# A transformer layer pair and a hybrid layer on one core: VectorE makes all low parts of the first block, a one-operation mask, and a new order of calls

## The chip, the cores and the metric

The kernel runs on one core of a Trainium2 chip. The metric is the device time of one execution in microseconds (us). Its engines are TensorE (PE, matmuls and transposes into eight PSUM banks), VectorE (DVE), ScalarE (ACT), GpSimd (POOL) and SyncE (SP, which here issues the loads). Each runs its own instruction list strictly in order, and they wait for each other through semaphores. DVE and ACT read PSUM; POOL doesn't.

## The reference

Two blocks in a row on 256 positions of 1024 columns, all in float32. The first block is two transformer layers:

```python
h = rms_norm(x, attn_norm_g[l]);  proj = h @ w_in[l]          # 1024 x 3656
# rotary q/k with a norm per head, then three mixers of 4 heads each:
moba = softmax(causal(q k)) v                                  # one block of 256: plain causal
diff = rms_norm((softmax(q1 k1) - lam * softmax(q2 k2)) v)     # differential
# dsa: per query the top 64 causal keys by an indexer of 8 heads, softmax over those
score = sum_h iw[h] * relu(iq[h] ik);  _, sel = top_k(causal(score), 64)
x = x + concat(moba, diff, dsa) @ w_out[l]
x = x + (silu(h2 @ w_gate[l]) * (h2 @ w_up[l])) @ w_down[l]    # 2816 wide, h2 = rms_norm(x)
```

The second block is one hybrid layer: `z = h @ w_in_2`, a gated MLP over positions (`y_a`, with a layer norm), 16 heads of compressed, selected and window attention (`y_b`), a convolution and linear recurrence (`y_c`), then

```python
merged = sum_i sigmoid(mg_i) * (y_i @ w_br_i)
x = x + rms_norm_2(merged @ w_o, g_post_mix)
x = x + rms_norm_2((silu(f_gate) * f_up) @ w_ffn_out, g_post_ffn)   # f from rms_norm_2(x)
```

## The kernel before

**Three products for one.** A weight chunk of 128 x 2048 floats (4 k-tiles of 512 columns, 1 MB) is loaded by SP into `raw`. ACT rounds it to `whi` (`split_hi`, called `hi` in the first block and `hi2` in the second), and DVE subtracts to get the rest, `wlo` (`split_lo`, called `lo` and `lo2`). The activations, transposed by TensorE, are split alike into `_hi` (ACT, `turned_hi_copy`) and `_lo` (DVE, `turned_lo_copy`) of `hT`, `mixT` and `ffT`. `three` then issues hi x hi, hi x lo and lo x hi (lines 587, 588, 589). `raw`, `whi` and `wlo` are rings of three slots: chunk i is loaded when the low part of chunk i-3 is done, and rounded when TensorE has used chunk i-3. `lo_ready` counts low parts, `used` counts chunks used up.

**First block.** Each engine's list for a layer is written out by hand as a row of calls, and their order is the schedule. On TensorE `row_product(p, j, r)` is a quarter of projection p (k-half j, rows r of 128; 12 matmuls), `turn_heads(s, b)` transposes heads, `index_scores` makes the indexer's scores, `group_scores`, `group_turn` and `group_values` are attention group g = 0 to 3 (scores, transposed probabilities, values; 1 and 2 differential, 3 the one with the top 64 keys), `mix_turn(h, r)` transposes the mixers' outputs and `out_product(n, j, r)` multiplies them by `w_out`, from chunks 17 to 20. ACT copies (`copy_z`, `heads_copy`), exponentiates (`attend_exp`) and normalises (`square_heads`, `scale_heads`). POOL rotates (`rotate`). DVE masks (`attend_mask`, three tiles), picks the top keys (`topk_rounds(a, b)` in 8 rounds, `topk_mask`), and blends (`blend`, `diff_norm`). Of the low parts, POOL makes those of chunks 18 and 20 (line 548, `pool_lo`), and DVE passes their completion on with `lo_from_pool`. `topk_mask` is two operations:

```python
dve(eng.tensor_scalar(chosen[:, :], index[:, :], TAKEN / 2, NEG, ALU.is_gt, ALU.mult))   # line 1804
dve(eng.tensor_tensor(chosen[:, :], chosen[:, :], causal[:, :], ALU.add))                # line 1806
```

**Second block.** Product b has chunks (b, 0) and (b, 1), which TensorE consumes with `product_chunk(b, j)`, each for rows 0 and then rows 1 (24 matmuls). Products 13 to 19 alternate with attention groups i (`attend_turn` transposes their probabilities; DVE's `attend_copy` moves a third of these to SBUF); `mix_positions(r)` is the MLP over positions and waits for the layer norm that DVE finishes at line 2341. Product 13 reads `mixT` (half 0 of its k-tiles in (13, 0), half 1 in (13, 1)) and waits for all four low parts of it (`turned_lo` 32). Around products 23 to 25 DVE does the recurrence (lines 2404 to 2421), which ends in `yc_lo`, the low part of `y_c`. Product 29 is the second half of `w_o`: its banks are freed by DVE's `gained(n, r, ...)` (line 1703), which needs `both_gain`, the product of two gain rows, and `x` times a gain. POOL makes these (lines 576 and 578) once the gain row is loaded (`ffn_gain`, SP line 454, behind all loads of products up to 29) and `yc_lo` has come. Then `post_square` (ACT), `new_rows` (DVE, line 2450) and `turn_row_part` (TensorE, line 631) give the rows of the last feed-forward part, `ffn`. Its result leaves through `gain` products (line 1950), `post_add` (line 1903) and four stores.

## Time and profile before

| | |
|---|---|
| median of 3 runs | 1286.12 us (1285.91 to 1287.7) |
| profiled execution, its own time | 1285.88 us |
| its span, first to last instruction | 1283.9 us |
| outside the span | 1.98 us |
| mean granted TensorE clock | 0.993 of full speed |
| HBM read | 211.28 MB, 165 GB/s over the span |
| chain that ended last | PE 86%, DVE 5%, issue 4%, ACT 2%, DMA 1%, POOL 1% |

Times in the profile count from the span's start. TensorE's busy time is modelled: matmuls overlap, so a row's duration is longer than the distance from one matmul's start to the next, and what is lost shows as idle time in square brackets ahead of an instruction, with what ended it behind the arrow. The chain is followed back from the last instruction, at each step to what released it.

### The profile page before, as it was taken

To read this page: it belongs to the slowest core of one execution; us is meant where nothing else is said; L and a number is where in the kernel's file an instruction comes from. 1 tells how busy PE (TensorE), PEld (TensorE's weight loads), DVE (VectorE), ACT (ScalarE), POOL (GpSimd) and SP (SyncE) were. 2 spreads that over 40 slices of the span, in tenths; PEclk is the share of its full clock that TensorE was granted. 3 is DMA by queue.
4 is the path that set the end of the run, shared out by engine and by line. 5 is a ranking of instruction groups with operands and counts; after the bars stand their busy time and mean duration, and the time that the engine had idled before them with its cause. 6 is when DMAs were issued, how large, how long until landed. Compare 5 with 4: busy or idle time off the path is not lost.

```text
span 1283.9 us, 16912 instructions
## 1 busy us (share of the span) xinstructions
PE 1254.1 (98%) x6430; PEld 1057.1 (82%) x6430; DVE 820.9 (64%) x983; ACT 663.4 (52%) x981; POOL 194.3 (15%) x162
## 2 busy tenths in 40 slices
PE   8999999999999999999999999999999999999998
PEld 6788888888887878888888899788997777888886
DVE  5898655545669866455457655866695677655444
ACT  5667463444466755434445644644547655634443
POOL 4884100001188620000000000000000003000000
PEclk9999999999999999999999998999999999999999
DMA  7533355556353344555564562343334455455551
GB/s 262 185 100 120 131 210 187 192 194 208 132 197 103 125 151 163 213 178 193 193 211 155 215 211 109 122 144 103 121 112 167 152 188 214 169 178 192 196 200 45
DMA packets 34219, 213.12 MB, mean 166 GB/s; under 512 B 4305, under 2 KB 5585, under 8 KB 11506
## 3 DMA queue, kind: packets, MB, share of 16 engines
q1 hardware_dynamic: 34098, 212.21, 46.9%
q8 instruction: 38, 0.62, 0.2%
q14 instruction: 19, 0.16, 0.0%
q0 software_dynamic: 64, 0.13, 0.0%
HBM read 211.28 MB, written 1.05 MB: 165 GB/s over the span
## 4 chain that ended last, share of the span: by engine, by line
PE 86%; DVE 5%; issue 4%; ACT 2%; DMA 1%; POOL 1%; POOLq 0%; DVEq 0%; ACTq 0%
PE bank L587 24%; PE bank L589 24%; PE bank L588 23%; PE bank L1002 3%; PE bank L694 2%; PE bank L753 2%; DVE wlo L1686 2%; PE bank L841 1%; PE bank L713 1%; ACT whi L1228 1%; DMA raw<-in_w_values 1%; DVE z L2166 1%; PE bank L615 1%; PE bank L678 1%; PE bank L1112 1%
## 5 line engine op out<-in xcount | busy, mean ns | idle before, releaser
L1686 DVE TENSOR_TENSOR wlo<-raw,whi 128x2048 fp32r<-128x2048 f32 (+4 forms) x197 | 442.4, 2250 | 246.8 <-ACT whi L1228 245.7
L1228 ACT ACTIVATE whi<-raw 128x2048 fp32r<-128x2048 f32 (+5 forms) x201 | 369.1, 1842 | 131.7 <-PE bank L589 124.0
L587 PE MATMUL bank<-whi,hT_hi 128*128 128x512 f32 (+4 forms) x1040 | 407.3, 392 | 6.2 <-DVE wlo L1686 3.0
L589 PE MATMUL bank<-whi,hT_lo 128*128 128x512 f32 (+4 forms) x1040 | 398.2, 383 | 0.0
L588 PE MATMUL bank<-wlo,hT_hi 128*128 128x512 f32 (+4 forms) x1040 | 397.8, 382 | 0.0
L587 PEld LDWEIGHTS bank<-whi,hT_hi 128*128 128x128 f32 x1040 | 196.6, 189 | 45.7 <-issue 6.8
L589 PEld LDWEIGHTS bank<-whi,hT_lo 128*128 128x128 f32 x1040 | 196.4, 189 | 36.3
L588 PEld LDWEIGHTS bank<-wlo,hT_hi 128*128 128x128 f32 x1040 | 196.9, 189 | 32.9
L587 PE MATMUL bank<-whi,mixT_hi 128*128 128x512 f32 (+1 forms) x248 | 96.5, 389 | 7.6 <-issue 3.9
L589 PE MATMUL bank<-whi,mixT_lo 128*128 128x512 f32 (+1 forms) x248 | 94.6, 381 | 0.0
L588 PE MATMUL bank<-wlo,mixT_hi 128*128 128x512 f32 (+1 forms) x248 | 94.5, 381 | 0.0
L587 PE MATMUL bank<-whi,ffT_hi 128*128 128x512 f32 x240 | 93.7, 390 | 0.0
L589 PE MATMUL bank<-whi,ffT_lo 128*128 128x512 f32 x240 | 93.5, 390 | 0.0
L588 PE MATMUL bank<-wlo,ffT_hi 128*128 128x512 f32 x240 | 93.4, 389 | 0.0
L1351 ACT ACTIVATE sqr<-bank,ssq 128x256 f32<-128x256 f32 x66 | 31.1, 473 | 88.0 <-PE bank L589 88.0
L1360 ACT ACTIVATE ffT_hi<-bank 128x256 fp32r<-128x256 f32 x60 | 19.8, 382 | 101.0 <-PE bank L841 101.0
L587 PEld LDWEIGHTS bank<-whi,mixT_hi 128*128 128x128 f32 (+1 forms) x248 | 47.1, 190 | 18.0 <-issue 6.2
L1917 DVE SCALAR_TENSOR_TENSOR probs<-bank,ssq,sqr 128x256 f32<-128x256 f32 x66 | 31.4, 480 | 44.6 <-ACT sqr L1351 44.6
L589 PEld LDWEIGHTS bank<-whi,mixT_lo 128*128 128x128 f32 (+1 forms) x248 | 47.1, 190 | 9.0
L588 PEld LDWEIGHTS bank<-wlo,mixT_hi 128*128 128x128 f32 (+1 forms) x248 | 47.1, 190 | 8.0
L576 POOL TENSOR_TENSOR z<-x,headsT 128x1024 f32<-128x1024 f32 x2 | 6.9, 3462 | 309.0 <-DMA headsT<-in_rows 309.0
L589 PEld LDWEIGHTS bank<-whi,ffT_lo 128*128 128x128 f32 x240 | 45.1, 188 | 9.4
(284 smaller groups left out, 1509.4 us busy)
## 6 DMA issues: line engine op xcount, KB each, us to landing
raw<-in_ff_loop SPq DMA_DIRECT2D x90, 1024.0 KB, 4.8
raw<-in_w_groups SPq DMA_DIRECT2D x64, 1024.0 KB, 4.8
raw<-in_w_out SPq DMA_DIRECT2D x8, 1024.0 KB, 5.6
raw<-in_ff_first SPq DMA_DIRECT2D x6, 1024.0 KB, 4.8
raw<-in_w_values SPq DMA_DIRECT2D x8, 728.0 KB, 4.2
raw<-in_w_comp SPq DMA_DIRECT2D x4, 1024.0 KB, 6.9
raw<-in_ff_last SPq DMA_DIRECT2D x3, 1024.0 KB, 6.8
raw<-in_w_values SPq DMA_DIRECT2D x4, 736.0 KB, 7.4
```

The source lines that it names most:

```text
L587: eng.matmul(out, lhsT=hi, rhs=wh, start=start, stop=False)
L588: eng.matmul(out, lhsT=hi, rhs=wl, start=False, stop=False)
L589: return eng.matmul(out, lhsT=lo, rhs=wh, start=False, stop=stop)
L615: mm = eng.transpose(bank[6 + r][:, k * P:(k + 1) * P], src[:, r, c:c + P], ident[:, :])
L694: mm = eng.matmul(bank[2 + u][:, c:c + keys], lhsT=headsT[half, q(h), rows], rhs=headsT[half, k(h), 0:keys], start=True, stop=True)
L753: mm = eng.matmul(out, lhsT=probsT[:, r + kt, h * P:(h + 1) * P], rhs=v(kt, h), start=(kt == 0), stop=(kt == r))
L1002: mm = eng.matmul(out, lhsT=a[i % RING][:, w], rhs=hT[h][:, 4 * j + k, :], start=(j == 0 and k == 0 and n == 0 and c % 2 == 0), stop=(j == ...
L1228: eng.activation(whi[j][:, 0:n], raw[j][:, 0:n], ACT.Copy).then_inc(hi_ready, 1)
L1351: eng.activation(sqr[:, r * FF_STEP:(r + 1) * FF_STEP], out[r][:, 0:FF_STEP], ACT.Silu, scale=ssq[:, 4 + r:5 + r]).then_inc(silu_ready, 1)
L1360: eng.activation(dst[0][:, 0:2, r * P:(r + 1) * P], bank[6 + r][:, 0:2 * P].rearrange("p (k c) -> p k c", k=2), ACT.Copy).then_inc(ff_hi, 1)
L1686: eng.tensor_tensor(wlo[j][:, 0:n], raw[j][:, 0:n], whi[j][:, 0:n].bitcast(F32), ALU.subtract).then_inc(lo_ready, 1)
L1917: eng.scalar_tensor_tensor(out=probs[:, r, 0:FF_STEP], in0=out[r][:, FF_STEP:2 * FF_STEP], scalar=ssq[:, 4 + r:5 + r], in1=sqr[:, r * FF_S ...
```

## The change

The POOL subtractions and `pool_lo` are gone: DVE makes the low parts of chunks 18 and 20 as well. The mask of the top keys is one operation that gives 1 where a key is left out and 0 where it counts, and the addition of that mask to the scores multiplies it by -1e30 on the way. The lists of PE, ACT and DVE for a layer of the first block are written in another order. In the second block some calls of the lists change places.

```diff
         (SP, second block)
+                if (b, j) == (24, 0):
+                    eng.wait_ge(xc_ready, 8)
+                    eng.dma_start(ffn_gain, t["rows2"][3, :].partition_broadcast(P)).then_inc(ffn_gain_loaded, 16)
-            eng.wait_ge(xc_ready, 8)
-            eng.dma_start(ffn_gain, t["rows2"][3, :].partition_broadcast(P)).then_inc(ffn_gain_loaded, 16)
...
         (POOL, first block)
-                for i in (18, 20):
-                    j = i % RING
-                    eng.wait_ge(hi_ready, l * CHUNKS1 + i + 1)
-                    eng.tensor_tensor(wlo[j][:, :], raw[j][:, :], whi[j][:, :].bitcast(F32), ALU.subtract)\
-                       .then_inc(pool_lo, 1)
...
         (PE, last ffn, first chunk of gate and up)
-                            if r == 0:
-                                turn_row_part(norm, 1, 0)
-                                turn_row_part(norm, 1, 1)
-                            tile(r, 4, i + 1).then_inc(used if r else gu_ready, 1)
+                            tile(r, 4, i + 1, 0 if r else 2).then_inc(used if r else gu_ready, 1)
...
         (PE, first block: the lines of the list ahead of the first out_product)
-                row_product(7, 0, 1); turn_heads(5, 0); row_product(7, 1, 0); row_product(7, 1, 1)
-                turn_heads(5, 1); group_turn(2); mix_turn(0, 0); group_scores(3); mix_turn(0, 1)
...
+                row_product(7, 0, 1); row_product(7, 1, 0); mix_turn(0, 0); row_product(7, 1, 1); group_turn(2)
+                group_scores(3); mix_turn(0, 1); out_product(0, 0, 0); group_values(2); group_turn(3)
...
         (PE, product 13)
-            eng.wait_ge(turned_lo, 32)
             three.act = mixT
+            eng.wait_ge(turned_lo, 30)
             product_chunk(13, 0)
             attend_turn(A + 2)
+            eng.wait_ge(turned_lo, 32)
             product_chunk(13, 1)
...
         (PE, product 29: rows 0 over both chunks, then rows 1)
-            product_chunk(29, 0); product_chunk(29, 1)
+            for r in range(RT):
+                eng.wait_ge(free[r], product(29))
+                for j in range(2):
+                    if r == 0:
+                        eng.wait_ge(lo_ready, done_at(T2, i + j))
+                    for k in range(4):
+                        if r and j and k == 2:
+                            turn_row_part(10, 0, 0)
+                            turn_row_part(10, 0, 1)
...
-            turn_row_part(10, 0, 0)
-            turn_row_part(10, 0, 1)
...
         (ACT, second block)
-            hi2(25, 0); branch_gate(24, 0); branch_gate(24, 1); hi2(25, 1)
+            hi2(25, 0); hi2(25, 1); branch_gate(24, 0); branch_gate(24, 1)
...
         (DVE)
-                dve(eng.tensor_scalar(chosen[:, :], index[:, :], TAKEN / 2, NEG, ALU.is_gt, ALU.mult))
-                dve.wait(eng)
-                dve(eng.tensor_tensor(chosen[:, :], chosen[:, :], causal[:, :], ALU.add))
+                dve(eng.scalar_tensor_tensor(out=chosen[:, :], in0=index[:, :], scalar=TAKEN / 2, in1=causal[:, :],
+                                             op0=ALU.is_gt, op1=ALU.is_gt))
...
-                        dve(eng.tensor_tensor(part, raw_scores, m.unsqueeze(1).to_broadcast([P, n, keys]), ALU.add))
+                            dve(eng.scalar_tensor_tensor(out=part, in0=m, scalar=NEG, in1=raw_scores, op0=ALU.mult,
+                                                         op1=ALU.add))
...
         (DVE, last ffn: the adds of rows 0 ahead of the third product with the gain)
                     for q, (n, r) in enumerate(((0, 0), (1, 0), (0, 1), (1, 1))):
-                        eng.wait_ge(squared, 4 + q + 1)
-                        dve(eng.tensor_tensor(mix[:, r, n * COLS:(n + 1) * COLS], bank[2 + 2 * n + r][:, :],
-                                              gain[:, n * COLS:(n + 1) * COLS], ALU.mult))
                         if q == 2:
...
+                        eng.wait_ge(squared, 4 + q + 1)
+                        dve(eng.tensor_tensor(mix[:, r, n * COLS:(n + 1) * COLS], bank[2 + 2 * n + r][:, :],
+                                              gain[:, n * COLS:(n + 1) * COLS], ALU.mult))
...
         (DVE, second block)
+            attend_copy(A)
             lo2(12, 0)
-            attend_copy(A)
...
-            lo2(12, 1)
             eng.wait_ge(gain_loaded, 96)
...
+            lo2(12, 1)
             attend_mask(A + 1, causal)
```

DVE's low parts of products 24, 25, 29 and 30 move as well; they are shown below. Three places in the lists follow.

DVE, first block, around the mask of the top keys (`index` is `chosen`; `probs<-bank,index` adds it to the scores of group 3). Before:

```order
L1867 SCALAR_TENSOR_TENSOR probs<-probs,coef 128x256 x2
L1796 MAX top<-index 128x8 x2
L1799 MATCH_REPLACE index<-top,index 128x128
L1799 MATCH_REPLACE index<-top,index 128x256
L1880 COPY probsT<-bank 128x256
L1804 TENSOR_SCALAR index<-index 128x384
L1806 TENSOR_TENSOR index<-index,causal 128x384
L1721 TENSOR_TENSOR mixT_lo<-bank,mixT_hi 128x4x128
L1824 TENSOR_TENSOR probs<-bank,index 128x512
L1828 TENSOR_REDUCE nmax<-probs 128x4
```

Of the change:

```order
L1807 SCALAR_TENSOR_TENSOR index<-index,causal 128x384
L1894 TENSOR_TENSOR dstat<-dstat,inv 128x4
L1899 SCALAR_TENSOR_TENSOR mix<-bank,dstat,sub_g 128x128 x4
L1859 RECIPROCAL inv<-sums 128x8
L1862 SCALAR_TENSOR_TENSOR coef<-sums,lam,inv 128x4
L1874 SCALAR_TENSOR_TENSOR probs<-probs,coef 128x128 x2
L1874 SCALAR_TENSOR_TENSOR probs<-probs,coef 128x256 x2
L1724 TENSOR_TENSOR mixT_lo<-bank,mixT_hi 128x4x128
L1887 COPY probsT<-bank 128x256
L1694 TENSOR_TENSOR wlo<-raw,whi 128x2048
L1830 SCALAR_TENSOR_TENSOR probs<-index,bank 128x512
```

The mask is made earlier, ahead of group 2's blend; the first low part of `mixT` no longer stands behind it, and the low part of chunk 17, which stood ahead of group 2's masks, now stands behind the copy of `probsT`.

DVE, second block, around the recurrence (`128x256 x8` are its eight scans). Before:

```order
L2148 TENSOR_TENSOR z<-z,scr 128x512
L2409 SCALAR_TENSOR_TENSOR z<-headsT,z 128x2x1024
L1686 TENSOR_TENSOR wlo<-raw,whi 128x2048
L2414 SCALAR_TENSOR_TENSOR headsT<-mix,z 128x256 x8
L1686 TENSOR_TENSOR wlo<-raw,whi 128x2048
L2418 TENSOR_TENSOR headsT<-headsT 128x2048
L1686 TENSOR_TENSOR wlo<-raw,whi 128x2048
L2421 TENSOR_TENSOR mixT_lo<-headsT,mixT_hi 128x2048
```

Of the change:

```order
L2155 TENSOR_TENSOR z<-z,scr 128x512
L1694 TENSOR_TENSOR wlo<-raw,whi 128x2048
L2417 SCALAR_TENSOR_TENSOR z<-headsT,z 128x2x1024
L1694 TENSOR_TENSOR wlo<-raw,whi 128x2048
L2422 SCALAR_TENSOR_TENSOR headsT<-mix,z 128x256 x8
L2425 TENSOR_TENSOR headsT<-headsT 128x2048
L1694 TENSOR_TENSOR wlo<-raw,whi 128x2048
L2428 TENSOR_TENSOR mixT_lo<-headsT,mixT_hi 128x2048
```

The low parts of (24, 1) and (25, 0) each move ahead of one step of the recurrence; that of (25, 1) and `yc_lo` keep their places.

DVE, second block, from the low part of chunk (29, 0) on (`z<-bank` and `mix<-bank` are `gained`, `z<-z,ssq` is `new_rows`, `hT_lo` is `turned_row_lo`). Before:

```order
L1686 TENSOR_TENSOR wlo<-raw,whi 128x2048
L1703 TENSOR_TENSOR z<-bank,headsT 128x512
L1703 TENSOR_TENSOR mix<-bank,gain 128x512
L1703 TENSOR_TENSOR z<-bank,headsT 128x512
L1703 TENSOR_TENSOR mix<-bank,gain 128x512
L1686 TENSOR_TENSOR wlo<-raw,whi 128x2048 x3
L1703 TENSOR_TENSOR z<-bank,headsT 128x512
L2450 SCALAR_TENSOR_TENSOR z<-z,ssq 128x512 x2
```

Of the change:

```order
L1694 TENSOR_TENSOR wlo<-raw,whi 128x2048
L1706 TENSOR_TENSOR z<-bank,headsT 128x512
L1706 TENSOR_TENSOR mix<-bank,gain 128x512
L1694 TENSOR_TENSOR wlo<-raw,whi 128x2048
L1706 TENSOR_TENSOR z<-bank,headsT 128x512
L1706 TENSOR_TENSOR mix<-bank,gain 128x512
L1694 TENSOR_TENSOR wlo<-raw,whi 128x2048
L1706 TENSOR_TENSOR z<-bank,headsT 128x512
L2457 SCALAR_TENSOR_TENSOR z<-z,ssq 128x512 x2
L1706 TENSOR_TENSOR mix<-bank,gain 128x512
L1711 TENSOR_TENSOR hT_lo<-bank,hT_hi 128x4x128 x2
L1694 TENSOR_TENSOR wlo<-raw,whi 128x2048
```

The low part of (29, 1) now stands between the two rows' `gained`, and that of the last feed-forward part's second chunk stands behind rows 0's new values and their low parts instead of ahead of them.

## Rows read from the trace of the kernel before

**Rows 1.** Waits of PE: line, releaser: us in total, times, longest.
```profile
PE bank L587 <- issue: 3.9, 2, 2.0
...
PE bank L694 <- ACT headsT L1284: 1.6, 2, 0.8
...
PE bank L739 <- ACT probsT L1322: 0.7, 1, 0.7
...
PE bank L694 <- DVE probsT L1880: 0.6, 2, 0.3
```

**Rows 2.** The page's group of `mixT` matmuls: busy us, mean ns | idle, releaser.
```profile
L587 PE MATMUL bank<-whi,mixT_hi 128*128 128x512 f32 (+1 forms) x248 | 96.5, 389 | 7.6 <-issue 3.9
```

**Rows 3.** Timeline, 118 to 127 us: start, duration, instruction [idle before, releaser].
```profile
125.32 0.47 PE L587 MATMUL bank<-whi,mixT_hi 128*128 128x512 f32 x1 [1.95 <-issue]
...
120.19 3.71 DVE L1804 TENSOR_SCALAR index<-index 128x384 f32<-128x384 f32 x1
123.93 0.56 DVE L1806 TENSOR_TENSOR index<-index,causal 128x384 f32<-128x384 f32 x1
124.53 0.69 DVE L1721 TENSOR_TENSOR mixT_lo<-bank,mixT_hi 128x512 fp32r<-128x512 f32 x1
...
119.15 4.53 POOL L548 TENSOR_TENSOR wlo<-raw,whi 128x2048 fp32r<-128x2048 f32 x1 [5.19 <-ACT whi L1228]
```

**Rows 4.** Stretches: length, busy us (instructions) of PE, PEld, DVE, ACT, POOL, clock, DMA.
```profile
105.00:156.00 51.00, 48.05 (x280) 41.88 (x278) 36.09 (x58) 29.96 (x73) 17.94 (x10) 0.97 0.41 154
125.30:129.70 4.40, 4.38 (x12) 3.48 (x13) 4.29 (x7) 2.79 (x13) 0.00 (x0) 0.61 0.02 4
847.10:852.70 5.60, 5.58 (x24) 4.56 (x25) 5.03 (x11) 4.23 (x17) 0.00 (x0) 1.00 0.11 47
1018.90:1036.90 18.00, 16.29 (x70) 12.83 (x70) 17.96 (x15) 8.59 (x6) 0.00 (x0) 1.00 0.42 147
```

**Rows 5.** DVE's scalar_tensor_tensor on a bank, by form: busy us, mean ns.
```profile
L2142 DVE SCALAR_TENSOR_TENSOR scr<-scr,bank 128x512 f32<-128x512 f32 x6 | 4.1, 684 | 4.3 <-PE bank L589 4.3
```

**Rows 6.** Timeline of PE, 813 to 848 us, instructions with idle time before.
```profile
816.95 2.31 PE L694 MATMUL bank<-headsT 64*128 64x128 f32 x16 [0.94 <-DVE probsT L1833]
822.77 0.45 PE L1144 MATMUL bank<-z,gain_c 128*128 128x256 f32 x1 [0.69 <-issue]
...
847.12 0.50 PE L587 MATMUL bank<-whi,mixT_hi 128*128 128x512 f32 x1 [1.56 <-DVE mixT_lo L1721]
```

**Rows 7.** Timeline of DVE, 813 to 823 us.
```profile
813.91 2.29 DVE L1686 TENSOR_TENSOR wlo<-raw,whi 128x2048 fp32r<-128x2048 f32 x1 [2.27 <-ACT whi L1228]
...
821.45 2.35 DVE L2341 TENSOR_TENSOR z<-z,gain 128x1024 f32<-128x1024 f32 x2
```

**Rows 8.** Timeline of PE, 1022 to 1092 us, instructions with idle time before.
```profile
1023.57 0.50 PE L587 MATMUL bank<-whi,hT_hi 128*128 128x512 f32 x1 [0.59 <-DVE wlo L1686]
1030.43 0.50 PE L587 MATMUL bank<-whi,hT_hi 128*128 128x512 f32 x1 [1.12 <-DVE wlo L1686]
...
1071.38 0.50 PE L587 MATMUL bank<-whi,mixT_hi 128*128 128x512 f32 x1 [0.75 <-DVE mixT_lo L1723]
1078.25 0.47 PE L587 MATMUL bank<-whi,mixT_hi 128*128 128x512 f32 x1 [1.14 <-DVE mix L1703]
...
1091.94 0.47 PE L587 MATMUL bank<-whi,hT_hi 128*128 128x512 f32 x1 [0.90 <-DVE hT_lo L1708]
```

**Rows 9.** Timeline of POOL and DVE, 1058 to 1077 us.
```profile
1065.50 6.88 POOL L576 TENSOR_TENSOR z<-x,headsT 128x1024 f32<-128x1024 f32 x2 [308.99 <-DMA headsT<-in_rows]
1072.35 4.44 POOL L578 TENSOR_TENSOR headsT<-gain,headsT 128x1024 f32<-128x1024 f32 x1
...
1065.88 4.24 DVE L1686 TENSOR_TENSOR wlo<-raw,whi 128x2048 fp32r<-128x2048 f32 x1
```

**Rows 10.** Timeline of DVE and PE, 1106 to 1110 us, instructions after one another.
```profile
1106.74 2.29 DVE L1686 TENSOR_TENSOR wlo<-raw,whi 128x2048 fp32r<-128x2048 f32 x1 [1.23 <-ACT whi L1228]
...
1109.62 0.47 PE L587 MATMUL bank<-whi,hT_hi 128*128 128x512 f32 x1
```

More of the change, by code:

```diff
@@ L1649, in _ @@
             hi2(29, 0)
-            for r in range(RT):
-                whole(28, r)
-                post_square(0, r, bank[r][:, :])
+            whole(28, 0)
+            post_square(0, 0, bank[0][:, :])
             hi2(29, 1)
+            whole(28, 1)
+            post_square(0, 1, bank[1][:, :])
             hi2(30, 0)
-            hi2(30, 1)
             whole(29, 0)
@@ L2406, in _ @@
             merge(23)
+            lo2(24, 1)
             dve.wait(eng)
@@ L2458, in _ @@
             new_rows(0, 1)
+            gained(1, 0, bank[0], mix, gain).then_inc(free[0], 1)
+            turned_row_lo(0, 0)
+            turned_row_lo(0, 1)
+            lo2(30, 1)
             dve(gained(1, 1, bank[1], z, both_gain, 4))
-            turned_row_lo(0, 0)
             dve.wait(eng)
@@ L2463, in _ @@
             new_rows(1, 0)
-            turned_row_lo(0, 1)
             new_rows(1, 1)
-            for r in range(RT):
-                gained(1, r, bank[r], mix, gain).then_inc(free[r], 1)
+            gained(1, 1, bank[1], mix, gain).then_inc(free[1], 1)
             turned_row_lo(1, 0)
```

126 lines of the change are left out of this document (67 added, 59 removed).

## The prediction

> **What bounds the kernel now.** I read the mean clock and the chain of waits first: the clock is near its full level and 86% of the chain is PE, so time comes off only where PE waits or runs at a lower clock. Then PE's waits sorted by what ended them, then the timeline of the other engines around each long wait.
>
> A wait costs PE a little more than its idle time: a `mixT` matmul's record lasts 0.389 us [rows 2], but 24 follow each other in 5.60 us, 0.233 apart [rows 4]. So an idle time that follows product matmuls stands for 0.389 - 0.233 = 0.16 more.
>
> In the first block the longest wait is ended by "issue", twice, 3.9 in all, 2.0 at most [rows 1]: one a layer, ahead of the first `out_product` [rows 3]. The reader should see there what came late: on DVE the comparison of the top keys took 3.71 us where the addition of the same size took 0.56, and `mixT_lo`, which the `out_product` needs, stands behind both and begins at 124.53 [rows 3]. POOL's low part ran from 119.15 to 123.68, and the comparison ended at 123.90, 0.22 later. And the stall has a second price: right after it 12 matmuls took 4.40 us at a granted clock of 0.61, where 24 took 5.60 at 1.00 [rows 4], so 4.40 - 2.80 = 1.6 us. The shorter waits of a layer are 0.8 ahead of `group_scores(1)` (ACT's copy), 0.7 ahead of group 1's values and 0.3 ahead of `group_scores(3)` [rows 1].
>
> In the second block DVE is late at several places, each because something less urgent stands ahead. A low part, 2.29 us, stands ahead of an attention copy and of the layer norm's additions [rows 7], for which PE waits 0.94 and 0.69 [rows 6]. Product 13 waits 1.56 for the low part of half 1 of `mixT` [rows 6], which its first chunk doesn't read. Around the recurrence DVE is busy 17.96 of 18.00 us [rows 4] and PE waits 0.59 and 1.12 [rows 8]. At product 29 PE waits 0.75, 1.14 and 0.90 [rows 8]; POOL's products begin as soon as the gain row has landed, at 1065.50, and end at 1076.79, a low part beside them took 4.24 instead of 2.29 [rows 9], and the 1.14 ends with DVE's `mix` behind `both_gain`.
>
> **First block, part by part, per layer.** The stall ahead of the first `out_product` gives 1.95 + 0.16, and the lower clock behind it 1.6: 3.7 together, if both go. For this `mixT_lo` must come in time: in the new order it stands behind the blend alone, the mask is done before, and the mask is one operation on the same size as the 0.56 addition [rows 3]. The new form of that operation has no row with these operands; a scalar_tensor_tensor of 128x512 with a bank takes 0.684 [rows 5], a tensor_tensor of that size 0.69 [rows 3], so I take 0.56, with 0.56 and 3.71 as bounds (the slow end only if POOL runs beside it, and its low parts are gone). The addition with the scale, 0.684 by the same rows, costs nothing more than now.
>
> DVE takes on two low parts, 2 x 2.29 = 4.6 us, and sheds 3.71: about 0.9 net. Between 105 and 156 it is busy 36.09 of 51.00 [rows 4], so 14 us stay free. That covers the amount, but not each place: a low part of 2.29 stands ahead of the masks of group 3 and of chunk 18's and 19's users. The cover is PE's queue of `row_product` and `out_product`, quarters of 12 x 0.233 = 2.8 us each; were it gone, each late low part would cost up to 2.29.
>
> The waits that stay or come: ahead of `group_scores(1)` and of group 1's values the same chains of copies stand as now, so 0.8 and 0.7 stay. `group_scores(3)` now comes directly behind `group_turn(2)`, without the `mix_turn(0, 0)` that stood between them; that is a copy's length without cover, 0.7 by the wait of the same kind at group 1 instead of 0.3: minus 0.45. For `group_scores(0)` and `group_turn(3)`, which have one call less ahead of them, I put 0.4 (bounds 0 and 0.8). Net 3.7 - 0.45 - 0.4 = 2.85 a layer, **5.7 for both**.
>
> **Second block.**
> - The copy and the additions go ahead of the low parts: 0.94 + 0.69, and 0.16 where products precede: 1.8. The two low parts come late by one such operation then, hidden behind attention work; without cover the loss is the same 1.2 (half of the 2.35 of both additions [rows 7]). I take 1.8.
> - Product 13's first chunk waits for half 0 only: 1.56 + 0.16 are gone. Behind it stands `attend_turn(A + 2)`, whose exponentials are as late as before while PE is 1.7 earlier by then; I put 0.6 for that (bounds 0 and 1.7): 1.1.
> - Recurrence: the low parts of (24, 1) and (25, 0) come ahead of 2.3 us of other work each: 0.59 + 1.12 + 2 x 0.16 = 2.0. What is late next is (25, 1): its low part ends no earlier than before, since the same work stands ahead of it on an engine that was full, and PE comes 2.0 earlier. I put 1.05 there, and 0.1 for ACT's branch gates, which stand behind a rounding now: 0.85 (bounds 0 and 2.0).
> - Product 29: gain row issued at product 24, so POOL's products can begin with `yc_lo`, at the end of the recurrence, and rows 0 and 1 are finished apart. Gone: 0.75 + 1.14 + 0.90 + 3 x 0.16 = 3.3. The last feed-forward part's low part of the following chunk ended at 1109.03, 0.6 before PE's matmul at 1109.62 [rows 10]; PE comes 3.3 earlier, this low part not by all of it, since the new rows' low parts stand ahead of it: 0.6 back. 2.7 (bounds 1.6 and 3.3).
> - Tail: one product of 128x512 (0.69 for that size [rows 3]) leaves the path of the last rows: 0.65.
>
> Sum: 1.8 + 1.1 + 0.85 + 2.7 + 0.65 = **7.1**. With the first block 12.8. The profiled execution took 1285.88, its span 1283.9 and 1.98 around it, which I leave as it is; it is 0.24 below the median of the three runs. Forecast: 1285.88 - 12.8 = **1273.1**.
>
> **The rivals.**
> *A* is the sum above. I give it 0.60, with 1269.5 to 1276.5 as its own range: the bounds of the unknown waits, added as if some go each way.
>
> *B*: a first-block stall of the old length remains. The mask isn't slow, but 3.7 a layer is lost at another place, for instance because the low part of chunk 17, now behind the blend, comes late for the first `out_product`; then the clock falls there as it does now [rows 4]. For it: the four low parts are packed behind one another; against: 14 us free. Two layers give back 7.4: 1285.88 - 5.4 = 1280.5. Chance 0.16. If the mask stayed slow without POOL beside it, that would be the same case: the change would not do what it says in the first block.
>
> *C*: the new order also removes the short waits. Then a layer gains 3.7 + 0.79 + 0.72 + 0.28 + 3 x 0.16 = 6.0 rather than 2.85, and the whole 19.1: 1266.8. For it: ACT's head copies and the eighth round of top keys stand earlier; against: the chains from `group_turn` to the values are the same. Chance 0.12.
>
> *D*: POOL's two products, released by `yc_lo` now, run beside DVE's low parts of product 26, and one takes 4.24 again [rows 9], 1.95 more; it eats the 0.85 of the recurrence: 1273.9, inside A's range. Chance 0.08. The Trainium skill, page "SBUF — State Buffer", section "SBUF: two separate sides", says that VectorE and GpSimd share one pair of ports as an exclusive lock: whichever starts first holds it for its whole instruction. That agrees with the 4.24 and with the 3.71 that ends 0.22 after POOL's; by that rule D would come true whenever POOL starts first.
>
> *E*, the slower side: VectorE becomes the bound of the first block's end. With the second block's 7.1 won, a layer would have to lose 4.9 more than today for 1285.88 - 7.1 + 9.8 = 1288.6. That is two low parts of 2.29 late one behind the other, with today's stall and low clock staying. The 0.7 busy share [rows 4] speaks against it, the order of the four low parts for it. Chance 0.04, half of it within 0.2%.
>
> **How the numbers follow.** 0.2% is 2.6 us, about what a measurement can tell from no change; faster means below 1283.5. A, C, D and B all end there, some of B's tail near it: faster 0.94, same 0.03, slower 0.03. The range has A and D whole and reaches towards both neighbours: 1268.0 leaves out most of C, 1279.5 the upper half of B and E, together about 2 in 10.
>
> **What would show it.** In the profile after: the mask's scalar_tensor_tensor at some 0.56 us; no idle time near 2 us ahead of the first `out_product`, and clock 1.00 in the stretch behind it; waits of 0.7 to 1.0 ahead of `group_scores(1)`, group 1's values and `group_scores(3)`. In the second block a wait of about 1 ahead of the matmuls of (25, 1), POOL's products right behind `yc_lo`, none of the 1.14 at product 29, and about 0.6 in the last part's second chunk of gate and up. The prediction is wrong if a wait of 2 us stands at another `out_product` (a late low part, B or E), if the mask takes over 1 us, or if the waits named as staying are gone (C).

## The result, and the profile after

| | before | changed |
|---|---|---|
| median of 5 runs each | 1286.29 us | 1280.45 us (1277.98 to 1280.99) |
| ratio, 95% interval | | 0.9948 (0.9937 to 0.9959) |
| profiled execution, span | 1285.88, 1283.9 | 1277.98, 1276.2 |

The change makes the kernel half a per cent faster; the forecast was 1273.1, and the range ended at 1279.5. The five runs fall into two groups, 1278.0 at a mean granted clock of 0.994 and 1280.5 to 1281.0 at 0.992; the profiled one is of the first. What the trace shows is therefore 4.9 us off the forecast, and the median 7.4.

The starts of TensorE's first product in each part, 343.52 and 674.09 us before, 342.93 and 674.74 after, say where: the first block (with the start) took 0.65 us more than before instead of 5.7 less, and the rest 601.5 instead of 609.8. The start, where TensorE waits for loads, differs a little from execution to execution. Counted from the first matmul of 128x368 behind it (24.81 before, 24.50 after) to the start of the third part, the first block takes 649.28 before and 650.24 after: 0.96 more. The first blocks of the experiments are compared in this way too.

The waits of PE after, in the columns of [rows 1]; L687 is `group_scores`, L580 the first matmul of a product, L706 `attend_turn`, L732 the values of a differential group:

```profile
PE bank L687 <- ACT headsT L1292: 6.0, 4, 2.2
PE bank L580 <- DVE wlo L1694: 4.3, 7, 1.1
...
PE bank L706 <- ACT probs L1313: 1.7, 2, 1.2
PE bank L732 <- DVE probsT L1887: 1.6, 2, 0.8
...
PE bank L687 <- DVE probsT L1887: 0.7, 1, 0.7
PE bank L687 <- ACT probsT L1330: 0.7, 1, 0.7
```

The 3.9 ended by "issue" of [rows 1] are gone, and the first line, 1.6 before, is 6.0 now. The timeline of DVE answers to [rows 3]: the mask takes 0.55, and `mixT_lo` comes when its input does, not behind a comparison.

```profile
115.51 0.55 DVE L1807 SCALAR_TENSOR_TENSOR index<-index,causal 128x384 f32<-128x384 f32 x1
...
120.91 0.69 DVE L1724 TENSOR_TENSOR mixT_lo<-bank,mixT_hi 128x512 fp32r<-128x512 f32 x1 [1.23 <-ACT mixT_hi L1251]
```

But other waits stand in the layer, some 55 us earlier. The timeline of PE, layer 0, then the same two calls in layer 1:

```profile
51.31 0.50 PE L580 MATMUL bank<-whi,hT_hi 128*128 128x512 f32 x1 [0.95 <-DVE wlo L1694]
...
69.97 2.31 PE L687 MATMUL bank<-headsT 64*128 64x128 f32 x16 [2.21 <-ACT headsT L1292]
...
88.72 1.09 PE L706 MATMUL bank<-ident,probs 128*128 128x128 f32 x8 [1.16 <-ACT probs L1313]
...
381.48 0.50 PE L580 MATMUL bank<-whi,hT_hi 128*128 128x512 f32 x1 [0.94 <-DVE wlo L1694]
...
400.13 3.92 PE L687 MATMUL bank<-headsT 64*128 64x128 f32 x16 [2.20 <-ACT headsT L1292]
```

51.31 is `row_product(3, 1, 0)`, 69.97 `group_scores(0)`, 88.72 the last tile of `group_turn(0)`. In layer 1 the 16 matmuls of `group_scores(0)` take 3.92 instead of 2.31. The stretches say why, with the columns of [rows 4]: `group_scores(0)` in layer 0, then in layer 1, then the 12 matmuls behind it in layer 1; and last the stretch of the first `out_product` of layer 0, now at full clock.

```profile
69.50:72.30 2.80, 2.33 (x17) 1.95 (x17) 2.73 (x4) 2.17 (x2) 2.72 (x3) 1.00 0.59 179
399.70:404.10 4.40, 3.97 (x17) 3.17 (x17) 4.26 (x5) 2.13 (x2) 4.24 (x5) 0.58 0.49 171
404.00:408.30 4.30, 4.30 (x13) 3.44 (x13) 4.16 (x9) 0.00 (x0) 2.39 (x2) 0.62 0.00 0
...
123.50:129.50 6.00, 5.86 (x36) 4.97 (x37) 5.90 (x8) 5.07 (x14) 0.00 (x0) 1.00 0.46 157
```

So the wait of 2.2 is there in both layers, and the lower clock behind it in one of them. It costs 3.92 - 2.31 = 1.6 at `group_scores(0)` and 4.35 (start to start) less the usual 2.85 = 1.5 behind it, 3.1 in all. A mean clock of 0.992 instead of 0.994 and 2.5 us more, as in three of the five runs, is what one more such stretch would give; no trace of those three is there, but in experiment 2 the profile of a slower run has the lower clock there in both layers.

Who is late? The timelines of ACT and DVE ahead of 69.97 (L1281 is `scale_heads`, L1292 `heads_copy`, L1299 `index_relu`; L1770 `head_sums`, L1781 the first operation of `index_sum`):

```profile
67.37 0.31 ACT L1281 ACTIVATE hln<-hss,eps 128x16 f32<-128x16 f32 x1 [3.21 <-DVE hss L1770]
...
67.83 0.58 ACT L1292 ACTIVATE headsT<-bank 128x512 f32<-128x512 f32 x1
68.31 1.08 ACT L1299 ACTIVATE probs<-bank 128x512 f32<-128x512 f32 x2
69.26 0.61 ACT L1292 ACTIVATE headsT<-bank 128x512 f32<-128x512 f32 x1
```

```profile
42.49 0.69 DVE L1770 TENSOR_REDUCE hss<-scr 128x8 f32<-128x512 f32 x1 [1.28 <-ACT scr L1276]
45.22 0.69 DVE L1770 TENSOR_REDUCE hss<-scr 128x8 f32<-128x512 f32 x1 [2.04 <-ACT scr L1276]
...
48.70 7.76 DVE L1694 TENSOR_TENSOR wlo<-raw,whi 128x2048 fp32r<-128x2048 f32 x3
56.38 0.48 DVE L1781 TENSOR_SCALAR index<-probs,z 128x128 f32<-128x128 f32 x1
...
66.65 0.69 DVE L1770 TENSOR_REDUCE hss<-scr 128x8 f32<-128x512 f32 x1
```

Read it backwards. TensorE waits for the copy at 69.26. ACT could have made it earlier, but stood 3.21 us in `scale_heads(l, 1)` for VectorE's sum at 66.65, with both copies queued behind. VectorE was late because it had idled 1.28 and 2.04 for the first head sums, then made three low parts in a row, and began the index sums at 56.38. The scores that these sums read come late as well: TensorE's first `index_scores`, now behind `row_product(3, 1, 0)`, begins at 54.25, before at 47.93, and ACT's `index_relu` of it at 55.62. From 20 to 45 us VectorE is busy 17.36 us, before 19.48; from 45 to 70 it is busy 24.29 of 25, before 21.58. First the changed kernel, then the kernel before:

```profile
45.00:70.00 25.00, 21.84 (x114) 16.82 (x112) 24.29 (x24) 14.67 (x24) 20.17 (x16) 1.00 0.32 122
```

```profile
45.00:70.00 25.00, 25.00 (x126) 19.08 (x125) 21.58 (x23) 16.34 (x24) 22.26 (x21) 1.00 0.38 131
```

The second block shows the waits that were forecast, of `attend_turn(A + 2)`, of (25, 1) and of the last `gate_up` (0.5, 1.12 and 0.45 of idle time), and none of [rows 8]'s last three:

```profile
849.89 1.09 PE L706 MATMUL bank<-ident,probs 128*128 128x128 f32 x8 [0.50 <-ACT probs L1313]
...
1031.82 0.50 PE L580 MATMUL bank<-whi,hT_hi 128*128 128x512 f32 x1 [1.12 <-DVE wlo L1694]
...
1102.52 0.50 PE L580 MATMUL bank<-whi,hT_hi 128*128 128x512 f32 x1 [0.45 <-DVE wlo L1694]
```

POOL's products now start as `yc_lo` ends, and a pair of low parts beside the second takes 7.19 instead of some 4.5, but no wait of PE follows:

```profile
1034.11 6.69 POOL L569 TENSOR_TENSOR z<-x,headsT 128x1024 f32<-128x1024 f32 x2 [276.83 <-DVE mixT_lo L2428]
1040.76 4.46 POOL L571 TENSOR_TENSOR headsT<-gain,headsT 128x1024 f32<-128x1024 f32 x1
...
1040.18 7.19 DVE L1694 TENSOR_TENSOR wlo<-raw,whi 128x2048 fp32r<-128x2048 f32 x2 [4.01 <-ACT whi L1236]
```

### The profile page after: what moved, and what is told of

It reads as the page before. It is cut to its first block, busy times and chain, and to the rows that moved or that the text cites. A ratio compares the mean times of both kernels' runs of the same rounds, so it can differ in the third digit from the quotient of the medians.

```text
span 1276.2 us, 16904 instructions
## 1 busy us (share of the span) xinstructions
PE 1249.3 (98%) x6430; PEld 1054.4 (83%) x6430; DVE 829.4 (65%) x985; ACT 662.3 (52%) x981; POOL 166.7 (13%) x158
## 3 DMA queue, kind: packets, MB, share of 16 engines
HBM read 211.28 MB, written 1.05 MB: 166 GB/s over the span
## 4 chain that ended last, share of the span: by engine, by line
PE 86%; DVE 9%; ACT 3%; issue 1%; POOL 0%; DVEq 0%; ACTq 0%; POOLq 0%
PE bank L580 24%; PE bank L582 24%; PE bank L581 24%; PE bank L687 3%; DVE wlo L1694 3%; PE bank L995 3%; PE bank L746 2%; DVE index L1783 1%; PE bank L608 1%; PE bank L706 1%; PE bank L835 1%; DVE z L2173 1%; ACT probs L1313 1%; ACT whi L1236 1%; PE bank L1105 1%
## 5 line engine op out<-in xcount | busy, mean ns | idle before, releaser
L1694 DVE TENSOR_TENSOR wlo<-raw,whi 128x2048 fp32r<-128x2048 f32 (+5 forms) x201 | 451.4, 2252 | 238.0 <-ACT whi L1236 236.0
L580 PE MATMUL bank<-whi,hT_hi 128*128 128x512 f32 (+4 forms) x1040 | 407.8, 392 | 6.4 <-DVE wlo L1694 4.0
L580 PEld LDWEIGHTS bank<-whi,hT_hi 128*128 128x128 f32 x1040 | 197.0, 189 | 45.4 <-DVE wlo L1694 7.2
L580 PE MATMUL bank<-whi,mixT_hi 128*128 128x512 f32 (+1 forms) x248 | 95.5, 385 | 0.3 <-DVE wlo L1694 0.3
L580 PE MATMUL bank<-whi,ffT_hi 128*128 128x512 f32 x240 | 93.7, 390 | 0.0
L580 PEld LDWEIGHTS bank<-whi,mixT_hi 128*128 128x128 f32 (+1 forms) x248 | 46.4, 187 | 9.4 <-DVE wlo L1694 1.4
L581 PEld LDWEIGHTS bank<-wlo,ffT_hi 128*128 128x128 f32 x240 | 45.1, 188 | 9.3
```

Source lines behind the costliest of these rows:

```text
L580: eng.matmul(out, lhsT=hi, rhs=wh, start=start, stop=False)
L581: eng.matmul(out, lhsT=hi, rhs=wl, start=False, stop=False)
L1694: eng.tensor_tensor(wlo[j][:, 0:n], raw[j][:, 0:n], whi[j][:, 0:n].bitcast(F32), ALU.subtract).then_inc(lo_ready, 1)
```

## The experiments

Each time below is a median; "before" is the kernel before on the same chip.

**1. The call that TensorE waits for.** In the changed kernel, ScalarE's list:

```diff
-square_heads(l, 1, 1); hi(5, 0); scale_heads(l, 1); heads_copy(l, 2, 0); index_relu(l, 4)
-index_relu(l, 5); heads_copy(l, 2, 1); hi(5, 1);
+square_heads(l, 1, 1); hi(5, 0); heads_copy(l, 2, 0); index_relu(l, 4)
+index_relu(l, 5); heads_copy(l, 2, 1); scale_heads(l, 1); hi(5, 1);
```

> The changed kernel with one call moved in ScalarE's list of the first block: scale_heads(l, 1) stands behind heads_copy(l, 2, 1) instead of ahead of heads_copy(l, 2, 0). Theory: in the changed kernel ScalarE stands 3.2 us in scale_heads(l, 1), for VectorE's sums, while the copy that group_scores(0) needs is queued behind it; TensorE waits 2.2 us there in each layer and then runs at the lower clock, in both layers or in one. Then the wait and the lower clock go: 2 x 2.28 + 3.1 less than the profiled 1277.98, so about 1270.3, with all runs within 0.5 us of each other. Rival: VectorE is late as such, and the wait only moves on, to the rotation of head set 1 and what reads it (a wait of over 1.5 us at another place of the layer, time 1276 or more).

Measured: 1280.53 (1277.67 to 1281.56), 0.9944 of before (0.9928 to 0.996). No gain. The timeline of PE in layer 0 shows the rival:

```profile
76.57 0.66 PE L915 MATMUL bank<-ident,z 128*128 128x128 f32 x4 [0.74 <-POOL z L521]
...
87.10 0.65 PE L706 MATMUL bank<-ident,probs 128*128 128x128 f32 x4 [1.19 <-ACT probs L1313]
...
88.91 1.09 PE L706 MATMUL bank<-ident,probs 128*128 128x128 f32 x8 [1.15 <-ACT probs L1313]
```

The wait ahead of `group_scores(0)` and the lower clock behind it are gone, and 0.74 for POOL's rotation, which hangs on the same head sums, and 1.19 for group 0's exponentials stand in their place; the 1.15 is there in both layers now. The runs still spread by 4 us, so that wait wasn't the only place where the clock falls in one execution and not in another.

**2. A low part ahead of the index key.** In the changed kernel, VectorE's list:

```diff
-head_sums(l, 0, 1); index_key(l); lo(3, 1); lo(4, 0)
+head_sums(l, 0, 1); lo(3, 1); index_key(l); lo(4, 0)
```

> The changed kernel with one call moved in VectorE's list of the first block: lo(3, 1) stands ahead of index_key(l). Theory: the wait of 0.95 us ahead of row_product(3, 1, 0) goes, but TensorE then comes 1.2 us earlier to group_scores(0), whose copy still hangs on ScalarE's scale_heads(l, 1), so that wait grows from 2.2 to about 3.4: no change, 1280.5 within 1 us. Rival: each wait is worth its own length: 2 x 1.19 less, a median of 1278.1.

Measured: 1277.92 (1277.15 to 1280.38), 0.9928 (0.9912 to 0.9943). The median suits the rival, but the trace neither: `turn_heads(1, 0)`, which now waits for the index key, takes over the wait at the same time,

```profile
51.31 0.44 PE L915 MATMUL bank<-ident,sqr 128*128 128x128 f32 x2 [0.92 <-DVE sqr L1749]
```

and the wait ahead of `group_scores(0)` is 2.02. The profile is of a run at 0.991 (1279.63 us), and in it `group_scores(0)` runs at the lower clock in both layers: the mean is 0.50, the lower level, from 71.0 to 75.5 us and 0.57 from 401 to 409. Four of six runs are at a clock of 0.993 or 0.994, the others at 0.991 and 0.992, where the changed kernel had two of five at 0.994; at 0.994 the two kernels are 1277.2 to 1277.5 and 1278.0. So the move is worth less than 1 us, and most of the difference of the medians is clock.

**3. Both moves.**

> Both of these moves together. Theory: once scale_heads(l, 1) is out of the way the 0.95 us ahead of row_product(3, 1, 0) are worth their full length: 2.4 us less than with the move of scale_heads alone, about 1267.9. Rival: the two add nothing to each other, within 0.5 us of the kernel with scale_heads moved alone.

Measured: 1279.64 (1276.68 to 1281.46), 0.9934 (0.9917 to 0.9951): 0.9 from the first of the two alone, so the rival's but for 0.4, and far from the theory's. Its profile has 1.30 ahead of `turn_heads(1, 0)` in layer 0, 0.54 for POOL and 1.19 and 1.15 for the exponentials.

**4. The second block alone.** The hunks of the second block and of the end on the kernel before, whose first block stays.

> The kernel before with the second block (and the end) of the change alone; its first block, POOL's low parts and the two-operation mask stay. Theory: the second block is worth what the two traces show between their third layers' starts and ends, 8.35 us, a little more than the 7.1 of the prediction: 1277.9. Rival: the second block gains only in that execution, or because it begins at another time: 1280 or more.

Measured: 1278.22 (1278.06 to 1279.49), 0.9931 (0.9915 to 0.9947). From the start of the third part to the end it takes 602.8 us, 7.0 less than before and 1.35 more than in the changed kernel's trace, whose second block is the same. That 1.35 stands ahead of everything that was changed there (the last section shows where it is from). From the sixteen matmuls of 128x256 that come ahead of the first changed call to the end it is 1283.9 - 791.98 = 491.9 us before, 1276.3 - 791.75 = 484.6 here and 1276.2 - 791.60 = 484.6 in the changed kernel. Their starts, before and here:

```profile
791.98 3.62 PE L1128 MATMUL bank<-headsT,probsT 128*128 128x256 f32 x16
...
791.75 3.62 PE L1129 MATMUL bank<-headsT,probsT 128*128 128x256 f32 x16
```

So the new calls of the second block bring 7.4, the same in both traces, and all that the whole change brings.

**5. The mask and the low parts in the old order.** The second block as changed; in the first block the lists of before, with POOL's subtractions gone, the scores' addition as in the change, and

```diff
-                dve(eng.tensor_scalar(chosen[:, :], index[:, :], TAKEN / 2, NEG, ALU.is_gt, ALU.mult))
-                dve.wait(eng)
-                dve(eng.tensor_tensor(chosen[:, :], chosen[:, :], causal[:, :], ALU.add))
+                dve(eng.scalar_tensor_tensor(out=chosen[:, :], in0=index[:, :], scalar=TAKEN / 2, in1=causal[:, :],
+                                             op0=ALU.is_gt, op1=ALU.is_gt))
...
-lo_from_pool(2 * l + 1); split_lo(t0, 19)
+split_lo(t0, 18); split_lo(t0, 19)
...
-lo_from_pool(2 * l + 2); split_lo(t0, FFN1)
+split_lo(t0, 20); split_lo(t0, FFN1)
```

> The second block as changed; in the first block the lists of the kernel before, but with the one-operation mask and with VectorE's low parts of chunks 18 and 20 in the places where it passed POOL's on. Theory: the mask and the low parts are worth what the prediction said (3.7 us a layer at the first out_product), and the new order of calls ate it: 1278.2, the time of the kernel with the second block alone, less 7.4, less a little for the four low parts: 1271 to 1272. Rival: two more low parts on VectorE cost what the mask gives, wherever they stand: 1276 or more.

Measured: 1270.56 (1270.3 to 1272.78), 0.9882 (0.9865 to 0.9899): faster than the changed kernel by 9.9 us by the medians and 8.5 by the ratios, each of which is to the kernel before in the same set of runs, and than the kernel with the second block alone by 7.7 (6.3 by the ratios). By the traces the first block, counted as above, takes 641.7 us here and 648.7 there, 7.0 less: 3.0 in layer 0 and 3.9 in layer 1. The waits of PE:

```profile
PE bank L689 <- ACT headsT L1295: 1.6, 2, 0.8
PE bank L734 <- ACT probsT L1333: 1.4, 2, 0.7
```

These are the short waits of [rows 1], and nothing ended by "issue" is left.

**6. The mask alone, 7. the low parts alone,** both with the old order and the new second block: of experiment 5 once the mask with its addition, once the low parts.

> As the kernel with the second block alone, with the one-operation mask; POOL keeps its low parts. Theory of the shared ports: the new operation has two operands in SBUF and stands behind POOL's subtraction like the old one, so it ends at 123.9 as before and only the second operation's 0.56 goes: a wait of about 1.4 us ahead of the first out_product, 1 us less in all, 1277. Rival, the form: the comparison was slow as a form of instruction, the new one takes 0.56 us beside POOL too, and the stall goes: 1271.

Measured: 1276.69 (1276.61 to 1277.14), 0.9925 (0.9912 to 0.9939). The timeline of DVE and POOL:

```profile
119.62 3.91 DVE L1821 SCALAR_TENSOR_TENSOR index<-index,causal 128x384 f32<-128x384 f32 x1
123.57 0.69 DVE L1738 TENSOR_TENSOR mixT_lo<-bank,mixT_hi 128x512 fp32r<-128x512 f32 x1
...
118.59 4.53 POOL L548 TENSOR_TENSOR wlo<-raw,whi 128x2048 fp32r<-128x2048 f32 x1 [5.21 <-ACT whi L1244]
```

> As the kernel with the second block alone, with VectorE's low parts of chunks 18 and 20; the mask keeps its two operations. Theory of the shared ports: without POOL beside it the comparison takes under 0.6 us, mixT_lo comes 3 us earlier and the stall goes, as with the mask changed too: 1271.5 to 1272.5. Rival, the form: it takes 3.7 us with POOL idle as well, and the stall stays: 1278 or more.

Measured: 1271.6 (1271.14 to 1271.69), 0.9884 (0.9868 to 0.99). DVE:

```profile
119.40 0.35 DVE L1816 TENSOR_SCALAR index<-index 128x384 f32<-128x384 f32 x1
119.78 0.56 DVE L1818 TENSOR_TENSOR index<-index,causal 128x384 f32<-128x384 f32 x1
120.47 0.69 DVE L1733 TENSOR_TENSOR mixT_lo<-bank,mixT_hi 128x512 fp32r<-128x512 f32 x1
```

The old comparison takes 0.35 with POOL idle, and the new operation 3.91 beside POOL's subtraction, ending 0.41 after it (118.59 + 4.53 = 123.12; 119.62 + 3.91 = 123.53). So the form was never slow; what ran beside it made it slow. The Trainium skill, page "SBUF — State Buffer", section "SBUF: two separate sides", says that of a VectorE instruction with two inputs in SBUF and a GpSimd instruction that reads SBUF, whichever starts first has the ports that they share for its whole length. The new operation and POOL's subtraction are such a pair, and their timeline agrees: POOL starts 1.03 earlier, and the 3.91 end 0.41 after it.

What each of the two changes is worth is read from the first block, from the first matmul of 128x368 (24.85 with the second block alone, then 23.76, 23.98 and 24.47 in experiments 6, 7 and 5) to the start of the third part (673.51, 671.82, 665.70 and 666.18): 648.7, 648.1, 641.7 and 641.7 us. Taking the low parts from POOL brings all of the 7.0; the one-operation mask brings 0.6 by itself and nothing on top. The medians of experiments 7 and 5 are 1.0 apart, but in their traces the two differ only behind these layers, where the kernels are the same.

**8. Three more moves in the new order,** on top of experiment 3:

```diff
-scale_heads(l, 2); hi(6, 0); attend_exp(A + 0, 0)
+hi(6, 0); attend_exp(A + 0, 0); scale_heads(l, 2)
...
-head_sums(l, 1, 0); index_sum(l, 2); index_sum(l, 3); head_sums(l, 1, 1); lo(5, 0)
+head_sums(l, 1, 0); head_sums(l, 1, 1); index_sum(l, 2); index_sum(l, 3); lo(5, 0)
...
-attend_mask(A + 0, causal, (1,)); head_sums(l, 2, 1); topk_rounds(1, 3); attend_mask(A + 0, causal, (2,)); topk_rounds(3, 5)
+attend_mask(A + 0, causal, (1,)); attend_mask(A + 0, causal, (2,)); head_sums(l, 2, 1); topk_rounds(1, 5)
```

> The changed kernel with five moves in the first block: scale_heads(l, 1) behind heads_copy(l, 2, 1) and lo(3, 1) ahead of index_key(l), as in the run of these two; scale_heads(l, 2) behind attend_exp(A + 0, 0) on ScalarE; on VectorE head_sums(l, 1, 1) directly behind head_sums(l, 1, 0), and the third mask tile of group 0 ahead of the rounds of top keys. Theory: in the run of the two moves TensorE waited for POOL's rotation of head set 1 (0.5) and for the exponentials of group 0 (1.2 and 1.15), because VectorE and ScalarE do less urgent work ahead; these go, some 2.8 us a layer, and the fall of the clock behind them: 1272 to 1274. Rival: VectorE is busy 24.3 of 25 us there, so what one call gains the next loses: 1278 or more.

Measured: 1279.56 (1279.32 to 1279.68), 0.9947 (0.9933 to 0.996): the rival's. The exponentials' waits are gone, and the low part behind the rounds of top keys, which begins at 89.86 and takes 2.08, is late instead; then the clock falls. The matmul that waits for it, and the stretch from 45 to 70 and that behind the wait:

```profile
91.99 0.43 PE L580 MATMUL bank<-whi,hT_hi 128*128 128x364 f32 x1 [2.50 <-DVE wlo L1694]
```

```profile
45.00:70.00 25.00, 24.07 (x130) 18.62 (x129) 24.39 (x24) 16.34 (x24) 20.36 (x15) 1.00 0.33 119
...
92.00:98.00 6.00, 5.26 (x25) 4.98 (x26) 5.90 (x14) 1.82 (x5) 5.84 (x8) 0.72 0.40 135
```

VectorE is as full as in the changed kernel (24.39 of 25). Whatever goes first, what goes last is late.

**9. The old order in the first part of a layer.** In the changed kernel, the lists of before up to `turn_heads(4, 1)` on TensorE, `square_heads(l, 3, 1)` on ScalarE and `head_sums(l, 3, 1)` on VectorE; the new ones behind. A part of TensorE's list and the beginning of VectorE's, where the loss was read above (`-` is the new order, `+` the old one that comes back):

```diff
-row_product(3, 1, 0); index_scores(l, 0); index_scores(l, 1); row_product(3, 1, 1)
+index_scores(l, 0); row_product(3, 0, 1); index_scores(l, 1); row_product(3, 1, 0)
...
-lo(1, 0); lo(1, 1); lambda_sums(l); lo(2, 0); lo(2, 1); lambda_value(l); lo(3, 0)
-head_sums(l, 0, 0); head_sums(l, 0, 1); index_key(l); lo(3, 1); lo(4, 0); lo(4, 1)
+lo(1, 0); lo(1, 1); lambda_sums(l); lo(2, 0); lo(2, 1); lambda_value(l); lo(3, 0); index_key(l)
+head_sums(l, 0, 0); lo(3, 1); head_sums(l, 0, 1); index_sum(l, 0); lo(4, 0); index_sum(l, 1)
```

> The changed kernel, with the lists of the kernel before in the first part of a layer: on TensorE from row_product(2, 0, 0) to the calls ahead of group_scores(1), on ScalarE to square_heads(l, 3, 1), on VectorE to the calls ahead of attend_mask(A + 1); behind that the new order. Theory: the new order loses in this first part alone, where VectorE first idles and then has no slack, and the rest of it does what was meant: 1270.6, the time with the old order throughout, plus the longer wait ahead of group_scores(3) (0.72 instead of 0.28, two layers): 1271 to 1272. Rival: the second part of the new order costs something as well, of the size of a low part: 1275 or more.

Measured: 1272.97 (1272.08 to 1273.68), 0.9898 (0.9883 to 0.9913): 7.5 less than the changed kernel by the medians, 6.4 by the ratios, and 1 above the theory's end. So the loss is in the first part of a layer, nearly all. The first block, counted as above, takes 650.2 us in the changed kernel, 643.1 here and 641.7 in experiment 5. So the new order of the first part costs 7.1, and 1.4 is left: 0.9 is the longer wait ahead of `group_scores(3)` in the two layers, 0.4 one ahead of `turn_heads(1, 0)` in layer 0 alone. The run puts back the lists of three engines together; which of the three costs most it doesn't tell.

**10. The first block alone.** The change without the hunks of the second block and of the end.

> The first block of the change alone (mask, low parts and new order), with the second block of the kernel before. Theory: the new order gives back all that the mask and the low parts bring, so this is no faster than the kernel before: within 1.5 us of its 1286.3, with runs some 2.5 us apart where the clock falls after the wait ahead of group_scores(0) or not. Rival: the two halves are worth the same with each other as alone only by chance, and this one is 3 us or more off.

Measured: 1286.74 (1283.79 to 1288.9), 1.0003 of before (0.9994 to 1.0012), from 1283.79 at a clock of 0.995 to 1288.9 at 0.991. No gain, as expected; the spread is twice what was expected. Its profile, of a run of 1287.6 us, shows one more source of it: in the old second block one wait of 2.63 stands at product 29, where the kernel before has 0.75 and 1.14, the mean clock from 1060 to 1100 us is 0.96 and not 1.00, and from the sixteen matmuls of 128x256 to the end it takes 494.1 us, not 491.9.

**11. The gain row late, 12. the old tail,** both on the kernel of experiment 5:

```diff
-                if (b, j) == (24, 0):
-                    eng.wait_ge(xc_ready, 8)
-                    eng.dma_start(ffn_gain, t["rows2"][3, :].partition_broadcast(P)).then_inc(ffn_gain_loaded, 16)
+            eng.wait_ge(xc_ready, 8)
+            eng.dma_start(ffn_gain, t["rows2"][3, :].partition_broadcast(P)).then_inc(ffn_gain_loaded, 16)
```

> As the kernel with the old order in the first block, with the gain row loaded at its old place, behind the loads of products up to 29. Theory: POOL's two products then run beside product 28 and 29 again, and the waits of 0.75 and 1.14 with what follows from them come back: 2 to 3 us more than 1270.6, 1272.6 to 1273.6. Rival: taking the two rows apart is what removed them, and the gain row's time is nothing: 1270.6 within 0.5.

Measured: 1274.07 (1273.03 to 1275.4), 0.9905 (0.989 to 0.992): 3.5 more by the medians, 3.0 by the ratios, whose intervals touch. The two waits of product 29 are back, 0.75 and 1.06:

```profile
1062.64 0.50 PE L582 MATMUL bank<-whi,mixT_hi 128*128 128x512 f32 x1 [0.75 <-DVE mixT_lo L1735]
...
1069.44 0.50 PE L582 MATMUL bank<-whi,mixT_hi 128*128 128x512 f32 x1 [1.06 <-DVE mix L1715]
```

That is 0.75 + 1.06 + 0.32 = 2.1 with the 0.16 for each, and the traces agree: from the sixteen matmuls of experiment 4 (here at 786.95, in experiment 5 at 784.17) to the end it is 486.55 and 484.43, 2.1 more. What else the times differ by stands ahead of them, where the kernels are the same. The place of one load, then, is worth 2.1 of the 3.3 that the forecast saw going at product 29.

> As the kernel with the old order in the first block, with the last products and additions in the order of the kernel before. Theory: one product of 0.69 us stands on the last chain again: 0.65 more, 1271.2, most clearly in the time from the last matmul to the end. Rival: VectorE has that time to spare anyway: no difference in that distance.

Measured: 1271.92 (1271.01 to 1272.72), 0.9889 (0.9874 to 0.9904), which can't be told from 1270.56 by the runs. From the start of the last matmul to the end it is 1270.8 - 1264.36 = 6.44 us, in experiment 5 1268.6 - 1262.91 = 5.69: 0.75.

## Why the prediction was wrong, step by step

**The stall ahead of the first out_product: right.** 3.7 us a layer were forecast; the old order without POOL's low parts and with the new mask takes 7.0 less for two layers (experiment 5: 3.0 in layer 0, where the clock didn't fall behind the stall in experiment 4, and 3.9 in layer 1, where it did). That POOL's subtraction made the comparison slow is shown by 0.35 without it and 3.91 for the new operation beside it. The forecast gave the gain to both changes together; it is the low parts' alone, and the one-operation mask adds nothing to them (experiments 6 and 7).

**The waits that come with the new order: here it failed.** The step read: for `group_scores(0)` and `group_turn(3)` "I put 0.4 (bounds 0 and 0.8)". `group_scores(0)` alone waits 2.2 us and then runs at the lower clock in some layers and executions, which costs 3.1 more, and two more waits of about 1 us stand before and behind it, the second in layer 0 alone. `group_turn(3)` has none. The bound was made from what stands ahead of a call on TensorE. What decided stood ahead of the copy on ScalarE, a call that waits for VectorE, and ahead of that sum on VectorE. In the kernel before the same chain was hidden by 0.3 us: the copy began at 67.91 and took 0.58, and `group_scores(0)` began at 68.75 without a wait. The chain of before, VectorE's sum, the copy and `group_scores(0)`:

```profile
64.92 0.69 DVE L1767 TENSOR_REDUCE hss<-scr 128x8 f32<-128x512 f32 x1
...
67.91 0.58 ACT L1284 ACTIVATE headsT<-bank 128x512 f32<-128x512 f32 x1
...
68.75 2.34 PE L694 MATMUL bank<-headsT 64*128 64x128 f32 x16
```

In the changed kernel the sum comes 1.7 later (66.65) and TensorE is ready 1.0 earlier (69.97 - 2.21 = 67.76); what ScalarE does between the sum and the end of the copy is 0.35 shorter. Less the 0.2 to 0.3 that were hidden, this makes the 2.2.

**VectorE's slack: read in the wrong stretch.** "14 us free" is true of 105 to 156, where the low parts were added. The list was rewritten from its start, and the stretch that filled up is 45 to 70, 24.3 of 25 us. I looked for the price where the operations were added, not where the calls were moved. That the new order of this part costs is shown by experiments 5 and 9. That VectorE is what is short there is read from the traces: in experiments 1, 3 and 8 each move only hands the wait to another of its results, or to an engine that stands behind one of them. It isn't isolated by a run: none puts back the list of one engine alone, TensorE's new list brings the index scores 6.3 us later, and the head sums for which VectorE idles 3.3 us were not moved behind a low part by themselves.

**The waits that stay** (`group_scores(1)` 0.78, group 1's values 0.78, `group_scores(3)` 0.72): as forecast, 0.8, 0.7, 0.7.

**A gain that I had not counted:** the index scores are issued in three pieces, 16, 8 and 8 matmuls (1.64 + 1.07 + 1.07 us from start to start), where before there were five with other calls between (1.09, 1.09, 1.07, 1.06, 1.06): 1.6 us a layer. TensorE comes earlier to `group_scores(0)` by it, and there it waits.

**The sum for the first block, layer 0 and layer 1.** The stall and the low clock behind it are gone, -3.7 and -3.7; `group_scores(3)` +0.4 and +0.4; ahead of `row_product(3, 1, 0)` +0.95 and +0.95; ahead of `group_scores(0)` +2.4 and +2.4 with the 0.16; the lower clock behind it 0 and +3.1; ahead of `group_turn(0)`'s last tile +1.2 and 0; the index scores -1.6 and -1.6. That makes -0.4 and +1.5; the traces show -0.3 and +1.2, where -2.85 was forecast for each.

**The second block: right in sum and nearly in its parts.** 7.1 were forecast; 7.4 measured in experiment 4 by the traces (8.9 by the runs, with an interval of 6.8 to 10.9: the old second block sometimes loses 2 us more, as in experiment 10). Of the waits that were to come, `attend_turn(A + 2)` costs 0.67 more from start to start than the same tile elsewhere (0.6 forecast), (25, 1) 1.28 (1.05), the last `gate_up` 0.6 (0.6). The tail gives 0.6 to 0.75 (0.65). POOL's collision came at the second low part of product 26, as in case D, and cost nothing, since no wait followed.

**The rivals.** B, with 0.16, came closest: the stall's length lost again at another place, 1280.5. The place that it named, a low part at an `out_product`, was wrong, and that its time is the median to 0.1 is luck, since the median hangs on how often the clock fell. E named VectorE, and the wrong end of the layer. The first block alone costs 0.4 us with an interval of -0.8 to 1.5 (experiment 10: 0.9994 to 1.0012 of 1286.0), where it was to bring 5.7.

## What to carry to other kernels

When a list is reordered, follow each result that another engine waits for back through the queues of all engines to where it starts, and look for the chains that are hidden by a few tenths of a microsecond now; those are the new waits. Measure an engine's slack in every stretch whose order changes, not only where work is added. And undo the reorder by itself: here the mask and the low parts are worth 7.0 us in the old order, and nothing in the new one; the fastest kernel of the study, 1270.56, is the old order of the first block with the new operations. Undo two operations that are changed together one by one as well: here one of them brought everything.
